# First attention: a step's turns ahead of its first scores on TensorE, and the combination ahead of the next minimum on VectorE

## The reference, cut to what matters

```python
def probs(qb, k):
    s = jnp.einsum('bqhd,bkhd->bhqk', qb, k).astype(jnp.float32) * scale + bias
    s = jnp.where(allowed, s, -jnp.inf)
    return jax.nn.softmax(s, axis=-1)

p = probs(qb1, k1) - lam * probs(qb2, k2)
return jnp.einsum('bhqk,bkhd->bqhd', p.astype(v.dtype), v)
```

## Time and profile before

| | us |
|---|---|
| median of 3 runs | 768.13 |
| lowest and highest | 766.93, 768.49 |
| the profiled execution | 767.41 |
| its span (first to last instruction) | 765.6 |
| TensorE busy in the span | 749.9 (98%) |
| VectorE busy | 608.6 (79%) |
| ScalarE busy | 318.1 (42%) |
| GpSimd busy | 348.9 (46%) |

### The profile page before, as it was taken

How to read it: one execution, slowest core, us unless ns; L and a number is a source line. 1 busy time by engine, 2 the same in 40 slices (tenths; PEclk the granted TensorE clock), 3 DMA queues, 4 the chain that set the end, 5 groups by cost and what they waited for, 6 DMA issues and landing times.

```text
span 765.6 us, 11907 instructions
## 1 busy us (share of the span) xinstructions
PE 749.9 (98%) x4174; PEld 634.6 (83%) x4174; DVE 608.6 (79%) x1301; ACT 318.1 (42%) x699; POOL 348.9 (46%) x429
## 2 busy tenths in 40 slices
PE   8999999999999999999999999999999999999996
PEld 7756888888888899899888888887998998988886
DVE  5548999999999988978799999995767667535444
ACT  7447131131315657666420302237646455423222
POOL 5220222223538868841354456659998991300000
PEclk9999999999999999999999999999999999999999
DMA  7331121212210011040122121210202030313131
GB/s 275 123 103 38 42 55 42 56 42 55 73 52 2 1 42 42 2 111 15 42 56 56 41 56 42 67 30 29 55 29 70 15 85 1 97 56 101 64 110 55
DMA packets 24563, 44.57 MB, mean 58 GB/s; under 512 B 3076, under 2 KB 10936, under 8 KB 24376
## 3 DMA queue, kind: packets, MB, share of 16 engines
q1 hardware_dynamic: 23352, 42.76, 19.1%
q10 hardware_dynamic: 1152, 1.05, 0.4%
HBM read 35.40 MB, written 6.57 MB: 55 GB/s over the span
## 4 chain that ended last, share of the span: by engine, by line
PE 90%; DVE 3%; ACT 3%; issue 2%; DMA 1%; POOL 1%; SPq 0%; ACTq 0%; DVEq 0%; POOLq 0%
PE psum L1250 40%; PE psum L1351 12%; PE psum L1428 11%; PE psum L1333 5%; PE psum L1311 4%; PE psum L1314 4%; PE psum L1142 3%; PE psum L1170 3%; PE psum L1205 3%; PE psum L1188 2%; PE psum L1318 1%; PE psum L1366 1%; ACT probsT_B L967 1%; PE psum L1317 1%; DMA xs<-in_x 1%
## 5 line engine op out<-in xcount | busy, mean ns | idle before, releaser
L599 POOL TENSOR_TENSOR w_lo<-w_raw,w_hi 128x512 fp32r<-128x512 f32 x60 | 77.9, 1300 | 218.7 <-ACT w_hi L780 218.4
L1614 DVE MATCH_REPLACE8 score<-top,score 128x768 f32<-128x768 f32 (+5 forms) x176 | 157.3, 907 | 0.0
L1609 DVE MAX8 top<-score 128x8 f32<-128x768 f32 (+5 forms) x176 | 148.2, 910 | 1.0
L780 ACT ACTIVATE w_hi<-w_raw 128x512 fp32r<-128x512 f32 x60 | 37.6, 630 | 211.9 <-PE psum L1250 208.9
L956 ACT ACTIVATE probs<-psum,small 128x384 f32<-128x384 f32 (+7 forms) x128 | 94.9, 742 | 45.2 <-DVE small L1635 30.3
L1250 PE MATMUL psum<-w_hi,big_hi 128*128 128x512 f32 x256 | 99.6, 389 | 0.0
L1250 PE MATMUL psum<-w_lo,big_hi 128*128 128x512 f32 x256 | 99.6, 389 | 0.0
L1250 PE MATMUL psum<-w_hi,big_lo 128*128 128x512 f32 x256 | 99.6, 389 | 0.0
L1351 PE MATMUL psum<-v,probsT_B 128*128 128x64 f32 x576 | 74.3, 273 | 2.4 <-ACT probsT_B L967 1.5
L1351 PEld LDWEIGHTS psum<-v,probsT_B 128*128 128x128 f32 x576 | 70.1, 191 | 7.9 <-issue 4.0
L1250 PE MATMUL psum<-big_hi,w_hi 128*128 128x512 f32 x192 | 74.8, 390 | 0.0
(11 more groups left out here) (188 smaller groups left out, 1596.9 us busy)
## 6 DMA issues: line engine op xcount, KB each, us to landing
w_raw<-in_w_in SPq DMA_DIRECT2D x62, 256.0 KB, 2.7
xs<-in_x SPq DMA_DIRECT2D x8, 512.0 KB, 6.6
k_high_twice<-k_high_twice SPq DMA_DIRECT2D x16, 256.0 KB, 3.7
xres<-in_x SPq DMA_DIRECT2D x8, 512.0 KB, 4.3
out_y<-y_out SPq DMA_DIRECT2D x8, 384.0 KB, 3.0
w_tail<-in_w_out SPq DMA_DIRECT2D x10, 256.0 KB, 2.8
bias_scratch<-bias_row SPq DMA_DIRECT2D x1, 2304.0 KB
bias<-bias_scratch SPq DMA_DIRECT2D x12, 128.0 KB, 3.0
```

Of the source, the lines that this page charges most:

```text
L599: pool.tensor_tensor(lo[:, 0:cols], w_staged(n)[:, 0:cols], hi[:, 0:cols].bitcast(f32), ALU.subtract).then_inc(w_lo_made, 1)
L780: act.activation(w_parts(n)[0][:, 0:cols], w_staged(n)[:, 0:cols], ACT.Copy).then_inc(w_hi_made, 1)
L1609: ins = dve.max(top8[:, i - SEL0, :], sc)
L1614: ins = dve.match_replace(sc, top8[:, i - SEL0, :], sc, TAKEN)
```

## The change

On TensorE, in the first attention only, the turns of step s-1 are issued ahead of scores(s+1, 0) instead of behind it. On VectorE, in steps 1 to 30 of the first attention, far_min(s+1, 0) is issued behind combine(s) instead of ahead of invert(s); in step 0 the old order stays. No instruction is added or dropped, and no wait is added to an instruction: each keeps its own. The second attention keeps its order.

```diff
@@ -1375,8 +1375,8 @@
                 for s in range(STEPS + lag):
                     t = s - lag
                     qs = quads[ph, t] if t >= 0 else []
-                    if s + 1 < STEPS:
-                        scores(ph, s + 1, 0)
+                    if ph == 1 and s + 1 < STEPS:
+                        scores(1, s + 1, 0)
                     if t == 0:
                         pe.wait_ge(bank_moved, moved[(A_GROUPS, B_GROUPS)[ph][-1] + 1])
                     if ph == 0 and s == STEPS:
@@ -1384,6 +1384,8 @@
                         rest_of_query(Q0 + 4, 0)
                     for quad in qs[0:2]:
                         turn(ph, t, quad)
+                    if ph == 0 and s + 1 < STEPS:
+                        scores(0, s + 1, 0)
                     if ph == 0 and s == STEPS:
                         rest_of_query(Q0 + 4, 1)
                     if ph == 0 and s < STEPS:
@@ -1715,11 +1717,13 @@
             for s in range(STEPS):
                 if s >= 2:
                     finishA(s - 2)
-                if s + 1 < STEPS:
-                    far_min(0, s + 1, 0)
+                if s == 0:
+                    far_min(0, 1, 0)
                 invert(0, s)
                 factor(s)
                 combine(s)
+                if 1 <= s < STEPS - 1:
+                    far_min(0, s + 1, 0)
                 if s + 1 < STEPS:
                     far_min(0, s + 1, 1)
             finishA(STEPS - 2)
```

## The result

| | us |
|---|---|
| median before (4 runs beside the change) | 767.97 |
| median of the changed kernel (4 runs) | 782.38 |
| its lowest and highest | 781.94, 782.60 |
| ratio, with its 95% interval | 1.0188 (1.0176 to 1.0201) |
| span of the profiled execution, before and after | 765.6, 780.1 |

The changed kernel is 14.4 us slower; the forecast was 784.0 with a range of 774 to 790. In the changed kernel every line behind the edit on TensorE stands two lower in the file, so L1635, L1669, L1685, L1694 and L1704 of before are now L1637, L1671, L1687, L1696 and L1706.

The account below looks back on a forecast made before the run. TensorE's own work was taken to bound the first attention. The chain's 15.0 us more plus 1 us for narrow steps made 16 us more, 783.4 on the profiled execution and 784.1 on the median; predicted 784.0, range 774 to 790.

Parts of the forecast that it names:

- What bounds the kernel: First attention: TensorE's own work is the bound, and any order can win no more than 1.2 to 4.8 us.
- The turns cost nothing: TensorE, first attention: turns ahead of the scores set at 0, with 1.2 to 4.8 us as best case.
- a chain closes: From exp(s, 1) through combination and minimum to exp(s+1, 1): 138.4 us against 121.8, 16.6 more if operations last as before.
- the scaled stretch: 14.2 us of lengthening beside GpSimd, times 0.89 for the longer stage: 12.6, making 136.8 us, 15.0 more.
- fixed part: Delays between successive operations from one step's exp(s, 1) to the next: 0.90 us a step, 27.9 over 31 steps.
- The stretch stays: VectorE's combinations still wait out whole GpSimd instructions under an exclusive port lock; 12.6 us of lengthening stays in the new order.
- The narrow steps: First attention, few keys: TensorE's 3.02 and 3.25 us exceed about 2.5 to 2.8 of VectorE and ScalarE; 1 us added.
- Everything behind moves by the same amount: After the first attention: all later work shifts equally, and VectorE's selection keeps 5.73 us of slack at the second attention.
- What would show it: First attention: blocks 35 to 37 us, last steps 28 to 30, TensorE waits 15 and more, combinations 32 to 36.
- The stretch goes: Rival, first attention: delayed combinations fall into GpSimd's gaps; 2.4 to 9 us more, 771 to 777; chance 0.16 (2.4 to 13).
- Not slower: Rival, first attention: TensorE's work in hand covers the delay, 763 to 768 us; chances 0.05 within 0.2%, 0.03 faster.
- More: Rival, first attention: the clock falls, or narrow steps give no credit with full GpSimd lengthening: 20.6 more, 789; above 790: 0.04.

Follow-up runs that it names:

- the late squares: Changed kernel with ScalarE's squares of step s-2 put behind exp(s+1, 1) instead of ahead of it: 781.95 us.
- the small split: GpSimd splits only 8 of each 512 columns of the third head's queries and keys: 778.73 us in the changed kernel, 767.47 in the kernel before.
- its wide steps alone: Kernel before, with the minimum (s+1, 0) behind the combination only where the next step has more than 512 keys: 786.37 us, ratio 1.0241.

## Why the prediction was right, point by point

**What bounds the kernel.** Right. TensorE's own work was the bound, with 1.2 to 4.8 us to win at most, and no kernel tried here won more than can be told from no change.

**The turns cost nothing.** Right for the whole change, since their wait for the combination is 1.6 us in all. But I had tied it to the minimum being behind the combination in one clause and did not price the case without it: alone, this half costs 13.7 us. With the minimum moved it is a gain of 5.9 us over the other half alone, where I had set 0 with a best case of 4.8. The chain in the wide steps did not need this term; the narrow steps did.

**The minimum was hidden behind exp(s, 1), and a chain closes.** Right. From the start of exp(0, 1) at 248.29 to that of exp(31, 1) at 383.22 it is 134.9 us; forecast 136.8 with the scaled stretch, and 1 us for the narrow steps. Term by term, from the rows of after:

| term | forecast | measured |
|---|---|---|
| combinations | 35.6, less the scaling of the stretch | 34.8 - 0.5 = 34.3 |
| one minimum of each pair | 23.4 | 47.8 / 2 - 0.6 = 23.3 |
| exponentials | 46.6 | 47.1 - 0.9 = 46.2 |
| factors beyond the fixed part | 4.9, less the scaling | 12.2 - 7.0 - 1.1 = 4.1 |
| fixed part | 31 x 0.90 = 27.9 | 31 x 0.82 = 25.4 |
| waits for TensorE in narrow steps | 1 | 1.6 |
| ScalarE's move of a fill result | 0 | 1.4 |
| step 0 in the old order, step 1 without squares | 0 | -1.4 |
| sum | 137.8 (139.4 less 1.6) | 134.9, passed 134.9 |

The term that was mis-sized is the fixed part. I took 0.37 for the squares, up to the end of their last row. In the changed kernel that row too ends 0.38 after its exponential (267.84 against 267.46), but the next exponential starts before this end, at 267.75, and the link is 0.28. Two terms were left out, and cancel. A step's last link is longer where ScalarE's move of a fill result stands between the exponentials, at the end of each of the first three blocks. The timeline of ScalarE there:

```profile
316.43 0.58 ACT L956 ACTIVATE probs<-psum,small 128x384 f32<-128x384 f32 x1 [1.64 <-DVE small L1637]
...
317.29 0.58 ACT L860 ACTIVATE qT<-psum 128x512 f32<-128x512 f32 x1
317.77 0.58 ACT L956 ACTIVATE probs<-psum,small 128x384 f32<-128x384 f32 x1
```

exp(16, 1) comes 0.76 after the end of exp(16, 0) instead of 0.28, and three times 0.48 are 1.4 us. On the other side step 0 keeps its old order, which saves 1.1, and step 1 has no squares yet, which saves 0.3.

The 15 us more were also taken against the wrong length. 121.8 us is the time from turns to turns; between the same two exponentials 120.9 us passed before (247.76 to 368.69). By my own terms the forecast was 136.8 + 1 - 120.9 = 16.9 us more in the stage, and the chain grew by 14.0. So the way and the path are as forecast, while part of the closeness of 784.0 to 782.4 is luck: this slip and the fixed part were errors in opposite directions.

**The stretch stays.** Right, and it is now shown, not only argued. The combinations sum to 34.8 us and the factors to 12.2, where the undisturbed sums are 26.8 and 7.0, so the stretch is 13.2 us, 12.1 of it in the chain (the last step's factor lies outside); forecast 12.6. How it comes about, from step 19, GpSimd above VectorE:

```profile
335.15 1.30 POOL L606 TENSOR_TENSOR k_zero_low<-kT,k_high_twice 64x512 fp32r<-64x512 f32 x1
336.53 1.26 POOL L606 TENSOR_TENSOR kT_r<-kT,k_high_twice 64x512 fp32r<-64x512 f32 x1
...
335.42 1.05 DVE L1687 SCALAR_TENSOR_TENSOR small<-small 128x1 f32<-128x1 f32 x1
336.50 2.37 DVE L1696 SCALAR_TENSOR_TENSOR probs<-probs,small 128x1024 f32<-128x1024 f32 x1
```

The factor, one column wide, ends at 336.47 with the first subtraction (336.45), and the combination ends 1.08 after the second one (337.79). The Trainium skill, SBUF — State Buffer, section "SBUF: two separate sides", has this as an exclusive lock for a whole instruction; by that rule coming earlier gains nothing while GpSimd's instruction runs, and the trace agrees: the 0.30 us of the late squares are gone at the end of that combination. Bandwidth shared between the two would have left a part of them.

**The narrow steps.** Right, in mechanism and size: TensorE is the bound there. Two narrow steps of block 2 in the table by stretches have it busy all the time:

```profile
311.05:313.97 2.92, 2.92 (x25) 2.79 (x24) 1.84 (x6) 1.94 (x9) 0.62 (x2) 1.00 0.35 90
313.97:316.50 2.53, 2.53 (x19) 2.39 (x18) 2.25 (x6) 0.51 (x3) 1.72 (x3) 1.00 0.00 0
```

VectorE meets this bound in finishA, which waits for the weighing (L1351), and the reciprocals stand behind it:

```profile
311.26 0.35 DVE L1706 TENSOR_SCALAR o_tmp<-psum,small 128x128 f32<-128x128 f32 x1 [0.92 <-PE psum L1351]
311.53 0.15 DVE L1671 RECIPROCAL small<-small 128x2 f32<-128x2 f32 x1
```

The reciprocals come up to 0.52 us after the exponential instead of 0.12, together 1.6 us over seven steps, where I had taken 1.

**Everything behind moves by the same amount.** Right: the tail is 393.0 us in both, and the second attention starts on VectorE with the same slack as in the earlier trace rows:

```profile
539.74 0.43 DVE L1642 CUSTOM_DVE_ANT_0 psum<-psum,mask 128x256 f32<-128x256 f32 x1 [5.74 <-PE psum L1314]
```

**What would show it.** Blocks 2 and 3 (35.86, 36.82) and the last steps (29.97) are in their ranges, the combinations are 34.8, and the idle time ahead of the reciprocals is 0.9 to 1.3 us in wide steps, the upper end a little over the 1.2 that I gave. Two signs were off. The first block takes 33.28, not 35 to 37: against block 2 its combinations are 0.9 us shorter (8.6 against 9.5), and it has step 0 in the old order (1.1) and step 1 without squares (0.3). And TensorE's waits are nearly all at the scores; with the 1.5 to 1.6 at the turns they are 12.0 us by the matmuls and 15.8 by the weight loads, so the 15 us and more are met by the second figure only.

**The rivals.** "The stretch goes" has its test in block 2 with the small split: there the loss is 2.26 us instead of the 4.70 (35.86 less 31.16) of the full one. It didn't go by itself. "Not slower" fell with the closed chain; TensorE's work in hand did not cover it: in wide steps it waits up to 1.3 us for the banks of its scores (the longest by the matmuls). "More" did not occur: the granted clock is 1.00 in all four stretches.

## What to carry to other kernels

Before reordering an in-order engine, write down what the moved instruction was hidden behind, and follow from its new place the ring of waits that leads back to the same instruction one step later. If the sum round that ring is longer than the step of the engine that bounds the stage, each part of it is paid in every step, with all that contention adds; where an instruction waits out another engine's long instruction, or the bounding engine's own step is the longer one, shortening what is ahead of it in the ring gives nothing. And two halves of a reordering can each close a ring of their own (13.7 and 20.3 us here, 14.4 together), so the halves are priced together.

## What the runs showed of the hardware

The granted clock of TensorE fell for some microseconds in three of the profiled executions: with the combination alone moved, with its wide steps alone, and with the squares late. In the first of them TensorE did nothing from 341.99 to 343.80 and resumed; then its clock fell (stretches of 1 us, the granted clock is the third figure from the right):

```profile
345.00:346.00 1.00, 1.00 (x7) 1.00 (x6) 0.93 (x3) 0.60 (x1) 0.00 (x0) 0.57 0.00 0
346.00:347.00 1.00, 1.00 (x3) 0.77 (x3) 1.00 (x2) 0.60 (x1) 0.00 (x0) 0.50 0.00 0
347.00:348.00 1.00, 1.00 (x4) 0.75 (x3) 0.02 (x1) 0.95 (x4) 0.00 (x0) 0.50 0.02 8
```

0.50 is the lower of its levels, 1.2 GHz. A wait of 3.06 us in the same execution, up to 257.88, and one of 2.05 with the turns alone moved were followed by no fall. With the squares late it fell to 0.50 from 323 to 326, after waits of 0.40 and 1.10 us, and in the changed kernel it stayed at 1.00 after waits of 0.13 and 1.10 at the same place. So the length of the last wait alone doesn't tell.

What a fall cost is seen where VectorE wants scores made at the lower clock. With the combination alone moved, exp(21, 1) comes 1.56 us after exp(21, 0) instead of 0.28, a loss of 1.3. With the squares late step 17 lasts 5.93 us, where it lasts 5.60 in the changed kernel; but step 18 lasts 5.96 for 6.22, and block 3 takes 36.85 us against 36.82 with the clock at 1.00. How much of the 788.31 us is the clock's stays open; its four executions don't suggest that it is much: of them the one with the highest mean clock, 0.997, took 788.42 us, and the two with the lowest, 0.991, took 788.21 and 788.58.
